# GpSimd's subtraction for a weight's low half: one instruction of 1024 columns, or four of 256

## The reference, cut to what matters

```python
x = first_block(x, ...)      # rmsnorm, one wide projection, pooling mixer + sliding-window attention, gated output,
                             # then: up = conv3(h @ w_up); x + (silu(gate) * val) @ w_down      (D_FF = 2816)
x = second_block(x, ...)     # 16 meta tokens; gated delta rule (4 heads) + full attention (8 heads), output projection,
                             # then: f = relu(u @ w_up)**2 @ w_down                             (D_FF_2 = 4096)
```

## Time and profile before

| | us |
|---|---|
| three runs: median (lowest to highest) | 1461.04 (1457.8 to 1462.58) |
| the profiled execution's own time | 1459.13 |
| its span, first to last instruction | 1457.3 |
| PE busy | 1375.3 (94%) |
| DVE busy | 736.2 (51%) |
| GpSimd busy | 764.9 (52%) |
| ACT busy | 433.8 (30%) |

### The profile page before, as it was taken

One profiled execution on the slowest core, in us unless ns is written; L12 is line 12 of the kernel. 1 busy time (PEld: TensorE's weight loads), 2 busy tenths in 40 slices (PEclk: granted clock), 3 DMA queues, 4 the chain that ended last, 5 costly groups with the idle time before them and its releaser, 6 DMA issues.

```text
span 1457.3 us, 19846 instructions
## 1 busy us (share of the span) xinstructions
PE 1375.3 (94%) x7304; PEld 1113.5 (76%) x7304; DVE 736.2 (51%) x1119; ACT 433.8 (30%) x842; POOL 764.9 (52%) x442
## 2 busy tenths in 40 slices
PE   7999999899999999999889999888989999999996
PEld 5777777678888887887878886647867888888885
DVE  7888766734544546114678885495643111211113
ACT  4353444423212212112345455344523111111111
POOL 5444534266666666664535433304265666667662
PEclk9999999999999999999999999999999999999998
DMA  5322211133322222222121111000032223323321
GB/s 193 101 87 72 88 58 59 44 101 104 101 90 97 101 95 93 100 87 87 62 69 44 49 54 54 20 1 2 8 109 72 97 91 101 100 88 101 101 86 58
DMA packets 31882, 113.83 MB, mean 78 GB/s; under 512 B 3536, under 2 KB 3920, under 8 KB 31696
## 3 DMA queue, kind: packets, MB, share of 16 engines
q1 hardware_dynamic: 31680, 112.85, 22.9%
q10 hardware_dynamic: 144, 0.18, 0.0%
HBM read 110.92 MB, written 2.10 MB: 78 GB/s over the span
## 4 chain that ended last, share of the span: by engine, by line
PE 85%; DVE 8%; ACT 4%; issue 2%; DMA 0%; DVEq 0%; SPq 0%; ACTq 0%
PE ps L1065 40%; PE ps L1279 18%; PE ps L1416 6%; ACT arena L575 3%; PE ps L1084 3%; PE ps L1098 2%; PE ps L1299 1%; PE ps L1390 1%; PE ps L1119 1%; PE ps L1220 1%; DVE arena L2146 1%; DVE arena L1744 1%; PE ps L1371 1%; PE ps L1182 1%; PE ps L1520 1%
## 5 line engine op out<-in xcount | busy, mean ns | idle before, releaser
L489 POOL TENSOR_TENSOR w_lo<-raw,w_hi 128x1024 fp32r<-128x1024 f32 x204 | 514.5, 2522 | 61.0 <-ACT w_hi L575 45.1
L483 POOL TENSOR_SCALAR w_hi<-raw 128x1024 fp32r<-128x1024 f32 (+1 forms) x188 | 202.2, 1076 | 526.7 <-PE ps L1065 175.6
L1065 PE MATMUL ps<-h_hi,w_hi 128*128 128x512 f32 x928 | 369.2, 398 | 5.2 <-DVE arena L1773 2.8
L1065 PE MATMUL ps<-h_lo,w_hi 128*128 128x512 f32 x928 | 362.3, 390 | 0.0
L1065 PE MATMUL ps<-h_hi,w_lo 128*128 128x512 f32 x928 | 362.2, 390 | 0.0
L1065 PEld LDWEIGHTS ps<-h_hi,w_hi 128*128 128x128 f32 x928 | 174.6, 188 | 51.8 <-issue 10.2
L1065 PEld LDWEIGHTS ps<-h_lo,w_hi 128*128 128x128 f32 x928 | 174.6, 188 | 38.3 <-issue 2.9
L1065 PEld LDWEIGHTS ps<-h_hi,w_lo 128*128 128x128 f32 x928 | 174.5, 188 | 36.8
L575 ACT ACTIVATE arena<-ps 128x512 f32<-128x512 f32 (+6 forms) x199 | 95.3, 511 | 237.0 <-PE ps L1119 62.7
L575 ACT ACTIVATE arena<-arena 128x512 f32<-128x512 f32 (+6 forms) x192 | 102.0, 535 | 213.3 <-DVE arena L2394 134.2
L1279 PE MATMUL ps<-g_hi,w_hi 128*128 128x512 f32 x400 | 155.7, 389 | 0.9 <-DVE arena L2005 0.9
(11 more groups left out here) (284 smaller groups left out, 1859.4 us busy)
## 6 DMA issues: line engine op xcount, KB each, us to landing
raw<-in_w_stream SPq DMA_DIRECT2D x204, 512.0 KB, 3.4
out<-xT SPq DMA_DIRECT2D x8, 256.0 KB, 2.1
xT<-in_x_t SPq DMA_DIRECT2D x1, 1056.0 KB, 8.1
xT<-in_x_t SPq DMA_DIRECT2D x1, 792.0 KB, 6.0
C<-in_cst SPq DMA_DIRECT2D x1, 576.0 KB, 9.6
arena<-in_cst SPq DMA_DIRECT2D x1, 528.0 KB, 4.4
xT<-in_x_t SPq DMA_DIRECT2D x1, 264.0 KB, 3.7
arena<-in_pos SPq DMA_DIRECT2D x1, 256.0 KB, 4.0
```

Of the source, the lines that this page charges most:

```text
L483: pool.tensor_scalar(w_hi[j][:, k0:KT, :], raw[j % 2][:, k0:KT, :], 1.0, 1.0, ALU.mult, ALU.mult).then_inc(S["pool_step"], 1)
L489: pool.tensor_tensor(w_lo[j][:], raw[j % 2][:], w_hi[j][:], ALU.subtract).then_inc(split_done[j], 1)
L1065: last = mm(dst[p], w[:, k, :], h[:, k, cols], start=(k == 0 and n == 0), stop=(k == KT - 1 and n == 2))
```

## The change

The subtraction is done in four instructions of two k-slices (256 columns) each, one behind the other with no wait between them; the last raises `split_done`. For the first round of the stream (units 0 to 3) it stays one instruction of 1024 columns. What is computed and where it is put is the same.

```diff
-                    pool.tensor_tensor(w_lo[j][:], raw[j % 2][:], w_hi[j][:], ALU.subtract).then_inc(split_done[j], 1)
+                    n = KT if isinstance(i, int) and i == 0 else 2
+                    for k in range(0, KT, n):
+                        low = pool.tensor_tensor(w_lo[j][:, k:k + n, :], raw[j % 2][:, k:k + n, :], w_hi[j][:, k:k + n, :], ALU.subtract)
+                    low.then_inc(split_done[j], 1)
```

## The result

| | before | changed |
|---|---|---|
| median (lowest to highest), 4 runs each | 1459.42 us (1456.47 to 1462.58) | 1445.08 us (1443.36 to 1446.17) |
| ratio to before, 95% interval | | 0.9896 (0.9874 to 0.9917) |
| a second series (a_again below, 6 runs), ratio | | 0.9907 (0.988 to 0.9934) |
| the profiled execution's own time | 1459.13 us | 1444.77 us |
| its span | 1457.3 us | 1441.0 us |

The kernel became faster by 14.3 us between the medians and by 15.2 us by the ratio (0.0104 x 1459.42). The forecast was 10.5. The direction is as predicted. The size is larger.

The account below looks back on a forecast made before the run. PE, busy 1375.3 of 1457.3 us, sets the end together with its 82 us of idling. Seven idle-time terms summed to 10.55 us, giving 1450.5 against the median of 1461.04; range 1445 to 1459, the forecast's own 1446 to 1454.

Parts of the forecast that it names:

- the clock's term: PE's low clock stretch at 757 to 763 us: put at nothing, with 3 us either way in the range.
- The price of a piece: A GpSimd subtraction of 256 columns takes 0.69 us, 0.13 of it fixed; four take 2.76 instead of 2.35.
- the fixed cost per instruction: Rival, chance 0.04: small subtractions have more fixed time, 0.5 us, so dense DVE stretches lose; 1467 us.
- the resource kept over instructions: Rival, chance 0.03: GpSimd holds the shared resource across instructions without waits, four pieces acting as one; 1463 us.
- Dense and single: DVE beside a subtraction: dense instructions gain only 0.5 us a subtraction, a single one is released up to 1.66 us earlier.
- Complete exclusion: Rival, chance 0.07: no part of GpSimd's and DVE's instructions overlaps; 1459.3 us, no measurable change.
- dense stretches give nothing: Rival, chance 0.12: seams cost what earlier release brings, only 4.45 us remain; 1456.6 us.
- Terms 3 to 7: PE's idle at 144.98, 274.85, 757.60, 801.70 with 812.85, and 920.19 us shrinks by 1.0, 1.5, 0.95, 3.2 and 1.0 us.
- Term 2: PE's idle at 132.16 us, behind two dense subtractions (rotary embedding): 0.3 of 2.11 us gained.
- Term 1: Start, 28 to 50 us, where PE waits twice for L1773: 2.6 of 2.84 us gained.
- I put all of this at nothing: GpSimd's 82 us of added time, hidden by its idle 526.7 us and four buffers, costs PE nothing.

Follow-up runs that it names:

- a_again: The changed kernel run once more, unaltered, in a second series: 0.9907 of the kernel before, 1443.26 us.
- e2: Kernel before with 256-column pieces only in rounds 5 to 10 (pooled product and heads of the first block): 0.9969 of before, 1456.97 us.
- e1: Kernel before with 256-column pieces only in rounds 1 to 4 (the program's start): 0.9965 of before, 1456.42 us.
- e3: Kernel before with 256-column pieces only in rounds 28 to 33 (the second block's convolution): 0.9951 of before, 1454.14 us.
- e4: Kernel before with pieces only in rounds 11 to 27 and from 34 on (long products): 0.999 of before, 1458.93 us.
- e9: Kernel before with pieces only in rounds 1 to 10 and 28 to 33, GpSimd's unit 21 held for the pooled input's low part: 0.988, 1440.7 us.
- b_again: The kernel before run once more, unchanged, for a second trace: 1.0013 of before, 1461.19 us.

## Why the prediction was right in kind and short in size

The mechanism was right: DVE waits for the end of the GpSimd instruction beside it, and TensorE gets back the idle time that hung on it. The step that failed is the clock's term, put at nothing; it measured 6.2 us.

**The price of a piece** (0.69 us, the fixed part of 0.13) holds: 0.70 here, 0.42 and 1.25 for half and twice the size. With it fall the fixed cost per instruction (it decides from 0.25, measured 0.14) and the resource kept over instructions (DVE gets in at every seam, 1.14 us apart).

**Dense and single.** DVE's pitch of 1.14 us is the 1.12 of the prediction. Complete exclusion would give 0.70 + 0.69 = 1.39. By the Trainium skill, page "SBUF — State Buffer", section "SBUF: two separate sides", the engine that comes second fully blocks until the other's instruction is over. The waiting until the end is in the traces here (3.26 us for an L1914 beside a whole subtraction, 1.63 beside pieces), the fully is not, since about a quarter of a microsecond in each hand-over overlaps. The rival that dense stretches give nothing fell too: the idle at the start, the 2.47 and the 1.54 us are all gone.

**The idle terms.** Their sum was 10.55, PE's time not busy fell by 10.1 in the profiled pair and by 9.4 as a mean of two pairs. Terms 3 to 7 are within 0.6 us of what the rows show: 1.03 for 1.0; 1.89 less the 0.97 that comes back, 0.9, for 1.5; 0.95 for 0.95; 3.38 for 3.2; 1.28 for 1.0. Term 2 is 0.18 for 0.3. **Term 1, "I put 2.6 of the 2.84",** was taken from one execution in which the start had fallen well. That stretch and the two behind it are worth 5.4 us over seven traces, for 3.9, the clock's part in them included. The agreement of 10.1 with 10.55 in the first pair is in part luck: it holds 1.35 us less waiting at L1508, which is no work of the change (1.10 and 2.70 us in the two traces of before, 1.35 and 2.70 in those of the changed kernel), against the 1.34 us lost near 1070.

**"I put all of this at nothing"** (GpSimd's 82 us more) held in the 370 us of long products, 0.04 us, and failed at one place, where it cost 1.34 us. I had looked whether GpSimd stays ahead of PE. I had not looked whether its last instruction before a DVE chain still misses that chain; it had missed it by 0.08 us.

**The clock, "I put nothing, and 3 us either way",** is the step that failed. PE's busy time fell by 6.2 us for the same work. I had looked at one low stretch only, the one behind the 4.07 us, and that one stayed. The one at 275 us, behind the 1.89, I had not read, and it went in the changed kernel, where the idle time before it is 0.97 (e2 shows it alone; e1, e3 and e4 keep it, e3 half as long; in e9 half of it is left behind the same 0.97). This is about 1.7 us: from the last score group to 326 us PE gained 0.73, though it had to give 0.97 back. The shorter low stretches at 690 and 914 us are behind some 1.4 of the 2.84 in the table (the rest is term 5 and 0.44 us of idling before it, at L1427) and about 1.1 of the 2.50 (without the 1.35 at L1508). Both are matters of the single execution: in a_again the one at 688 us has its full length and the one at 750 us half, and in b_again those at 700 and 761 us are the short ones. Why they are shorter or longer stays open: the idle in front of them is 3.78 us in both kernels at the one, and 2.21 at the other. That it is not fixed shows also in the kernel before itself, whose second trace has the full clock behind the same 2.21 us of idling, there at 930.18, where the first has 0.51:

```profile
930.00:936.00 6.00, 5.82 (x28) 3.98 (x28) 1.68 (x4) 1.66 (x3) 4.09 (x7) 1.00 0.00 0
```

So some 1.7 us of the clock's 6.2 go with the idle time closed at 275 us, in five traces of six. For the rest only the correlation is shown: the changed kernel's runs have the higher mean clock in both series, and the time follows the clock. Its cause stays open.

The account by means: 9.4 idle and 6.2 clock are 15.6 us of span, against 15.2 by the ratio.

## What to carry to other kernels

A long GpSimd instruction that reads the on-chip memory holds up the DVE instructions named here until its end, so where TensorE waits for DVE, cut it or hold it back; here 256 columns (0.70 us) were best, 512 too long to help and 128 too many for GpSimd. Check the cover twice: that GpSimd stays ahead of TensorE, and that its last instruction before each DVE chain still ends ahead of the chain. And when idle times of a microsecond or two close, read the granted clock behind each of them, split the span into TensorE's busy and idle time before and after, and take terms that hang on which instruction is hit from more than one execution.

## What the runs showed of the hardware that I had not expected

The prediction gave the rule for DVE instructions with two inputs, though it counted on L1765, which has one. DVE instructions with a single input wait too, if both sides lie in the on-chip memory: the TENSOR_SCALARs L1762, L1765 and L1767 of 512 columns take 0.43 us alone, 2.51 to 2.61 beside a whole subtraction and 0.84 beside pieces. The pair at L1773, of whose two inputs one comes from PSUM, takes 1.27 to 1.29 us in every trace of the start, beside a subtraction or not.

The same kernel has more than one course. Where it falls is settled in the first 35 us and shows 100 us later as 132.16 or 135.04 us, and at 163.66 in e3 as 2.12 us of idling that no other trace has. It explains part of why the runs of before spread over 10 us (1454.49 to 1464.34).

TensorE's clock followed idle times of under 2 us: behind 1.89 us at 275 us it went to 1.2 GHz in all six traces that have it, behind 0.97 at the same place it stayed at 2.4 in five of six.
